# Hybrid decoder layer: last down step by token halves, a later start of Pool's third weight sums, two attention tiles begun at the second pair, compress sum one group later

## The reference

```
h = rmsnorm(x);  x = x + 0.5 * swiglu(h, w_gate, w_up, w_down)      # FFN 0, inner width 2816
h = rmsnorm(x);  x = x + concat(gated_delta_net(h), sparse_attention(h)) @ w_out
h = rmsnorm(x);  x = x + 0.5 * swiglu(h, ...)                        # FFN 1
return rmsnorm(x)                                                    # final norm, then y goes out
```

## Time and profile before

| | |
|---|---|
| median of 3 runs | 1134.47 us (1133.08 to 1135.31) |
| the profiled execution | 1136.39 us, span from first to last instruction 1134.6 us |
| PE busy | 1087.9 us (96%) |
| DVE busy | 777.8 us (69%) |
| ACT busy | 448.7 us (40%) |
| POOL busy | 449.8 us (40%) |
| mean granted TensorE clock | 0.985 |
| DMA | 98.45 MB, 87 GB/s on average |

### The profile page before, as it was taken

One profiled execution on the slowest core, in us unless ns is written; L12 is line 12 of the kernel. 1 busy time (PEld: TensorE's weight loads), 2 busy tenths in 40 slices (PEclk: granted clock), 3 DMA queues, 4 the chain that ended last, 5 costly groups with the idle time before them and its releaser, 6 DMA issues.

```text
span 1134.6 us, 20093 instructions
## 1 busy us (share of the span) xinstructions
PE 1087.9 (96%) x8476; PEld 942.7 (83%) x8476; DVE 777.8 (69%) x926; ACT 448.7 (40%) x628; POOL 449.8 (40%) x288
## 2 busy tenths in 40 slices
PE   6889999999999999899999899999989999999996
PEld 5789899989998888787787567888888899989985
DVE  5998379936986666544456387566997489937963
ACT  6543245413444334311223476343443144413431
POOL 0662169506822000213201299432561279306912
PEclk9999999999999999899999899999999999999998
DMA  6244233332323221123102001123223223322222
GB/s 225 74 124 146 75 108 94 133 100 87 102 84 116 94 77 69 38 74 115 39 31 63 21 2 39 31 82 106 67 88 111 84 103 111 126 98 78 100 84 75
DMA packets 33438, 98.45 MB, mean 87 GB/s; under 512 B 3536, under 2 KB 8144, under 8 KB 31696
## 3 DMA queue, kind: packets, MB, share of 16 engines
q1 hardware_dynamic: 33072, 97.26, 26.1%
q10 hardware_dynamic: 288, 0.08, 0.0%
HBM read 95.24 MB, written 2.10 MB: 86 GB/s over the span
## 4 chain that ended last, share of the span: by engine, by line
PE 87%; DVE 8%; ACT 3%; issue 2%; POOL 0%; DMA 0%; DVEq 0%; ACTq 0%
PE bank L586 24%; PE bank L587 24%; PE bank L588 24%; PE bank L1998 3%; PE bank L1753 1%; PE bank L1784 1%; PE bank L1769 1%; DVE hb_lo L710 1%; DVE w_lo L982 1%; DVE w_lo L905 1%; DVE cv L1498 1%; PE bank L2056 1%; DVE c_sb L1038 1%; PE bank L2053 1%; DVE act_lo L1077 1%
## 5 line engine op out<-in xcount | busy, mean ns | idle before, releaser
L586 PE MATMUL bank<-hb_hi,w_hi 128*128 128x256 f32 x1064 | 295.4, 278 | 13.2 <-DVE w_lo L905 9.3
L587 PE MATMUL bank<-hb_lo,w_hi 128*128 128x256 f32 x1064 | 294.5, 277 | 0.0
L588 PE MATMUL bank<-hb_hi,w_lo 128*128 128x256 f32 x1064 | 294.4, 277 | 0.0
L586 PEld LDWEIGHTS bank<-hb_hi,w_hi 128*128 128x128 f32 x1064 | 200.5, 188 | 14.9 <-issue 6.5
L587 PEld LDWEIGHTS bank<-hb_lo,w_hi 128*128 128x128 f32 x1064 | 200.5, 188 | 0.3
L588 PEld LDWEIGHTS bank<-hb_hi,w_lo 128*128 128x128 f32 x1064 | 200.3, 188 | 0.0
L586 PE MATMUL bank<-act_hi,w_hi 128*128 128x512 f32 x448 | 178.7, 399 | 9.9 <-DVE w_lo L918 9.9
L587 PE MATMUL bank<-act_lo,w_hi 128*128 128x512 f32 x448 | 178.1, 398 | 0.0
L588 PE MATMUL bank<-act_hi,w_lo 128*128 128x512 f32 x448 | 177.9, 397 | 0.0
L899 ACT ACTIVATE w_hi<-raw 128x1536 fp32r<-128x1536 f32 (+1 forms) x67 | 108.8, 1624 | 165.4 <-PE bank L588 165.4
L905 DVE TENSOR_TENSOR w_lo<-raw,w_hi 128x1536 fp32r<-128x1536 f32 (+1 forms) x67 | 158.1, 2360 | 16.0 <-ACT w_hi L899 15.3
(11 more groups left out here) (299 smaller groups left out, 1717.9 us busy)
## 6 DMA issues: line engine op xcount, KB each, us to landing
raw<-in_gate_up SPq DMA_DIRECT2D x43, 1024.0 KB, 5.4
raw<-in_w_in SPq DMA_DIRECT2D x13, 1024.0 KB, 4.9
raw<-in_down SPq DMA_DIRECT2D x8, 1024.0 KB, 5.1
raw<-in_down SPq DMA_DIRECT2D x16, 512.0 KB, 4.2
raw<-in_down SPq DMA_DIRECT2D x8, 768.0 KB, 4.3
raw<-in_w SPq DMA_DIRECT2D x8, 512.0 KB, 4.0
x<-in_x SPq DMA_DIRECT2D x4, 512.0 KB, 7.4
raw<-in_w_out SPq DMA_DIRECT2D x4, 512.0 KB, 4.6
```

Of the source, the lines that this page charges most:

```text
L586: pe.matmul(out_ap, wh, xh, start=first, stop=False)
L587: pe.matmul(out_ap, wh, xl, start=False, stop=False)
L588: return pe.matmul(out_ap, wl, xh, start=False, stop=last)
```

## The change

1. The last `Down` step of the second FFN is done for tokens 0 to 255, then for 256 to 511, each half in a bank of its own, with 256-column matmuls. Additions, squares, POOL's last addition, feature sums, root, reciprocal, broadcast, final multiplication and output DMAs are done per half: 16 multiplications and 16 DMAs of 256 tokens. PE does half 0's feature sums between the two output tiles of half 1. ACT takes a root of one number first. POOL adds the last tile but one per half, too.
2. In both FFNs POOL waits, before the sums of the sixth gate-up step, for the first DVE addition of the fourth one.
3. PE calls `pe_tile_start` for the first two token tiles right after the scores of the second pair, not ahead of their first value products.
4. `hid_sum` and `kcvc` stand one group number later.

```diff
-CMP_AT = {22: ("hid_sum",), 24: ("kcvc",), 26: ("scores", 0), 27: ("scores", 1), 30: ("scores", 2),
+CMP_AT = {23: ("hid_sum",), 25: ("kcvc",), 26: ("scores", 0), 27: ("scores", 1), 30: ("scores", 2),
...
+            if st is FFN[1][-1]:
+                pe_last_down(pe, st)
+                return
...
+        def pe_last_down(pe, st):
+            par = st.step % 2
+            for half in range(2):
+                t = tok_half(half)
+                for ab in range(2):
+                    for j in range(st.tiles):
+                        w = slice((ab * st.tiles + j) * P, (ab * st.tiles + j + 1) * P)
+                        mm = three_pass(pe, last_bank(ab, half), w_hi[:, par, w], w_lo[:, par, w],
+                                        act_hi[:, j, t], act_lo[:, j, t], j == 0, j == st.tiles - 1)
+                    mm.then_inc(last_part, 1)
+                    if half and not ab:
+                        pe_last_sum(pe, 0)
+            pe_last_bc(pe, 0)
+            pe_last_sum(pe, 1)
+            pe_last_bc(pe, 1)
...
+        def pe_last_sum(pe, half):
+            out = spare_bank(half)
+            pe.wait_ge(x_added, X_ADDED0[1] + KT * len(PARTS) - 2)
+            pe.wait_ge(last_summed, half + 1)
+            for src, first in ((sq_sum, True), (sq[:, 1, :], False)):
+                if not first:
+                    pe.wait_ge(last_sq, 2 * half + 2)
+                for i in range(2):
+                    t = 2 * half + i
+                    mm = pe.matmul(out[:, i:i + 1], src[:, t * P:(t + 1) * P], ones,
+                                   start=first and i == 0, stop=not first and i == 1)
+            mm.then_inc(last_ss, 1)
...
+        def dve_last(dve):
...
+            add(0, 0)
+            add(0, 1)
+            add(1, 0)
+            root(0)
+            add(1, 1)
+            for k in range(KT // 2):
+                scaled(0, k)
+            root(1)
+            for k in range(KT // 2, KT):
+                scaled(0, k)
+            for k in range(KT):
+                scaled(1, k)
+
+        def act_last(act):
+            st = FFN[1][-1]
+            act.activation(root_first, eps_col, ACT.Sqrt)
...
+            square(0, 0)
+            square(0, 1)
+            square(1, 0)
+            root(0)
+            square(1, 1)
+            root(1)
+
+        def pool_last(pool):
+            for half in range(2):
+                t = tok_half(half)
+                pool.wait_ge(last_sq, 2 * half + 1)
+                pool.tensor_tensor(sq_sum[:, t], sq_sum[:, t], sq[:, 0, t], ALU.add).then_inc(last_summed, 1)
...
             pool_first_sums(pool, FFN[f][PLAIN + 1])
+            pool.wait_ge(post_done, 5 * FFN[f][PLAIN].n + 1)
             for st in FFN[f][PLAIN + 2:]:
...
+            if i == 1:
+                pe.wait_ge(cmp_pt_evac, 2)
+                for t in range(TT):
+                    if TILE_AT[t] < 2:
+                        pe_tile_start(pe, t)
...
-                if i - PV_LAG == TILE_FIRST[t]:
-                    if i == PV_LAG:
-                        pe.wait_ge(cmp_pt_evac, 2)
-                    if TILE_AT[t] >= 2:
-                        pe.wait_ge(ocat_lo, TILE_AT[t] - 1)
+                if i - PV_LAG == TILE_FIRST[t] and TILE_AT[t] >= 2:
+                    pe.wait_ge(ocat_lo, TILE_AT[t] - 1)
                     pe_tile_start(pe, t)
...
-            for k in range(KT):
-                sp.wait_ge(y_ready, k + 1)
-                sp.dma_start(out[:, k, :], x[:, k, :]).then_inc(out_landed, 16)
+            for half in range(2):
+                t = tok_half(half)
+                for k in range(KT):
+                    sp.wait_ge(y_ready, half * KT + k + 1)
+                    sp.dma_start(out[:, k, t], x[:, k, t]).then_inc(out_landed, 16)
```

More of the change, by code:

```diff
@@ L881, in pe_down, with last_bank, spare_bank, tok_half @@
                                         act_hi[:, j, :], act_lo[:, j, :], j == 0, j == st.tiles - 1)
-                    if st is FFN[1][-1] and ab == 0:
-                        mm.then_inc(last_half, 1)
             mm.then_inc(step_done, 1)
+        def last_bank(ab, half):
+            return banks[4 * (FFN[1][-1].step % 2) + 2 * half + ab][:, 0:TOK]
+        def spare_bank(i):
+            return banks[4 * (1 - FFN[1][-1].step % 2) + i]
+        def tok_half(half):
+            return slice(half * TOK, (half + 1) * TOK)
@@ new lines, in pe_last_bc, with add, root, scaled @@
+        def pe_last_bc(pe, half):
+            pe.wait_ge(last_rstd, half + 1)
+            for i in range(2):
+                t = 2 * half + i
+                mm = pe.matmul(spare_bank(2 + half)[:, i * P:(i + 1) * P], rstd[:, t:t + 1].to_broadcast([P, P]), ident,
+                               start=True, stop=True)
+            mm.then_inc(last_bc, 1)
+        def dve_last(dve):
+            st = FFN[1][-1]
+            def add(half, ab):
+                k, t = 2 * st.at + ab, tok_half(half)
+                dve.wait_ge(last_part, 2 * half + ab + 1)
+                dve.scalar_tensor_tensor(x[:, k, t], last_bank(ab, half), 0.5, x[:, k, t], ALU.mult, ALU.add)\
+                   .then_inc(last_added, 1)
+            def root(half):
+                c = slice(2 * half, 2 * half + 2)
+                dve.wait_ge(last_rms, half + 1)
+                dve.reciprocal(rstd[:, c], rms[:, c]).then_inc(last_rstd, 1)
+            def scaled(half, k):
+                t = tok_half(half)
+                if k == 0:
+                    dve.wait_ge(last_bc, half + 1)
+                    dve.wait_ge(last_added, 2 * half + 2)
+                dve.scalar_tensor_tensor(x[:, k, t], x[:, k, t], norm_w[:, 3, k:k + 1],
+                                         spare_bank(2 + half)[:, 0:TOK], ALU.mult, ALU.mult).then_inc(y_ready, 1)
+            add(0, 0)
[10 more added lines that the diff above has]
+                scaled(1, k)
@@ L1022, in act_ffn @@
                     act_split_sums(act, then)
-                if isinstance(st, Down) and st.part == len(PARTS) - 1:
+                if isinstance(st, Down) and st.part == len(PARTS) - 1 and st is not FFN[1][-1]:
                     for k in (2 * st.at, 2 * st.at + 1):
@@ L1100, in dve_ffn @@
                     dve_split_sums(dve, then, 1)
-                if isinstance(st, Down):
+                if isinstance(st, Down) and st is not FFN[1][-1]:
                     for ab in range(2):
                         k = 2 * st.at + ab
[L1104 to L1107, removed]
+                        dve.wait_ge(step_done, splits(st.step) + 1)
                         dve.scalar_tensor_tensor(x[:, k, :], banks[4 * (st.step % 2) + ab][:, :], 0.5, x[:, k, :],
@@ L1122, in pool_sums @@
             pool_clear(pool, m)
-            for k in range(KT - 1):
+            for k in range(KT - 2 if m == 3 else KT - 1):
                 pool.wait_ge(sq_ready, (m - 1) * KT + k + 1)
```

33 lines of the change are left out of this document (23 added, 10 removed).

## The result

The changed kernel took 1126.16 us (median of 8 runs, 1122.70 to 1128.46), the kernel before beside it 1134.07 (8 runs, 1130.95 to 1136.60). The ratio is 0.9924, 95% interval 0.9908 to 0.9941: 8.6 us faster (6.7 to 10.4; the two medians by themselves lie 7.9 apart), where 14.6 were forecast. The profiled execution took 1126.86 us (span 1125.1), 9.5 less than the one of before.

The account below looks back on a forecast made before the run. PE was taken as the bound, busy 96% of the span, leaving waits, low clock and the tail to win. Terms 3.8 + 1.0 + 3.1 + 3.2 + 3.5 = 14.6 us off 1134.5 gave 1119.9, forecast 1120; range 1115 to 1126.

Parts of the forecast that it names:

- Pool's wait, first FFN: Sixth gate-up step, first FFN: PE's wait of 3.36 us becomes 2.4, worth 1.0 us (-0.5 to 2.2).
- Pool's wait, second FFN: Sixth gate-up step, second FFN: PE's wait falls from 5.4 to about 2.4 us; worth 3.8 us (1.5 to 5.5).
- compress sum: Mixer: PE's 1.49 us wait for evictions and 1.7 us of lower clock behind it go; 3.1 us (0.8 to 3.3).
- tile starts: Attention: two tile starts fit into PE's 4.47 us wait for the first exponentials; 3.2 us (1.2 to 4.2).
- tail: Kernel's end: half 0's chain finishes beside half 1's matmuls, so the last multiplication ends earlier; 3.5 us (0 to 4.5).
- rival E: Mixer: compress sum and tile starts both gain nothing because they find another wait; 1126.2 us, chance 0.04.
- C: FFN starts: Pool/VectorE lock time is only moved; 1123.2 us, or 1126.9 with lower clock and low attention gain; together 0.18.
- A: The forecast itself, all places gaining as priced: 1119.9 us, chance 0.62.
- B: Tail bound by SP's output issues (16 x 0.65 us) or smaller transfers, its 3.5 us lost; 1123.4 us, chance 0.13.
- The half of the low clock behind this wait: Second FFN, behind PE's sixth-step wait: 1.5 us of lower clock may or may not come; half, 0.8 us, counted.
- the lost clock: Attention, behind the wait for exponentials: of 3.4 us lost to low clock, 0.4 us goes as idle time shrinks.
- I take DVE's pace: Output at the end: SP's 16 DMA issues were assumed to follow DVE's multiplications, not cost 0.65 us each (10.3 us).

Follow-up runs that it names:

- e1: The kernel before with only Pool's wait ahead of its sums added, in both FFNs: 1131.01 us, ratio 0.9967.
- e2: The kernel before with only the compress sum and its copies one group later: 1132.44 us, ratio 0.9974.
- e7: The changed kernel plus eight 512-wide matmuls of zeros behind the two early tile starts, filling the attention's remaining wait: 1121.66 us, ratio 0.9877.
- e4: The kernel before with only the last down step by token halves and halved output DMAs: 1131.57 us, ratio 0.9983.
- e10: The changed kernel with tile starts back at their old places and the attention's 4.5 us wait filled with 20 matmuls of zeros: 1123.63 us, ratio 0.9899.
- e8: The changed kernel with the last output in 8 DMAs of two tiles instead of 16 of one: 1124.06 us, ratio 0.9899.

## Why the prediction was right and wrong

| term | predicted | between the two profiles | alone on the chip (interval) |
|---|---|---|---|
| Pool's wait, first FFN | 1.0 | 1.6 | both: |
| Pool's wait, second FFN | 3.8 | 3.3 | 3.7 (1.9 to 5.6) |
| compress sum | 3.1 | 3.1 | 3.0 (1.0 to 4.9) |
| tile starts | 3.2 | -0.8 | -0.6 (-2.5 to 1.2) |
| tail (2.1 from the last `Down` step on) | 3.5 | 2.3 | 1.9 (-0.1 to 4.0) |
| sum | 14.6 | 9.5 | 8.0; all together 8.6 |

The direction was right, and three of the four places gave something; the size was not right, and 1126.16 lies just above the upper end of the range (1126). It is also rival E's number, 1126.2, and that is luck: E has the compress sum bring nothing, and it brought its 3.1. C's later time, 1126.9, lies outside the range that is said to hold C, and the chances of A, B, C and E add up to 0.97, not 0.96; neither bears on the forecast.

- **Pool's wait** held: the operations ahead of L1059 are back at 1.21 us, PE's wait at the sixth step is 2.03 us (2.4 predicted) in the second FFN and 1.01 in the first, and it did not come back at the seventh step. Rival C, 1.5 us in all because the stretches only move, lies below the interval of e1. The step's flaw: it took one profile's order of VectorE and Pool as certain. The predicted 4.8 against 3.7 alone is inside the interval; e2's trace shows how a loss there can be absent without the edit. The half of the low clock behind this wait, 0.8 of the 3.8, did not show: from PE's start at the sixth step to the first addition of the next `Down` step it is 41.47 us before, with the low clock, 41.34 in the changed kernel, without it but at TensorE's slower pace (0.118 us from matmul to matmul, last section), and 40.39 in e7, which has neither. The prediction's own 0.110 counts matmuls that reach over the ends of a window; the timelines show 0.113, which moves no term.
- **Compress sum** held in both halves, wait and clock, and the scores did not feel the later copies. Its clock half is luck in part: e4 had the wait and no low clock.
- **Tile starts: this step failed.** "With 2.0 instead of 4.5 us idle some of the 3.4 us of lost clock goes too: 0.4". The wait shrank as predicted (4.47 to 1.88), the two starts ran in 1.4 us each instead of 2.1 and 1.25, but the lost clock grew. The 3.4 us were priced by length and not by place: part of that spell lay in the wait, for nothing, and the step moved it onto products and got a longer one. The prediction has that low clock "just behind a wait", but in the trace of before it is already 0.50 from 642.90 on, 1.1 us ahead of the scores at 643.98 (0.80 in the earlier trace rows shows it too). The starts are worth 1.5 us with no low clock (e10 against e7), a term of 2.1 + 0.7 at mixed clock in the prediction. Why the spell was 10.2 us and not 6.8 is open. Rival E named the effect (nothing gained) with the wrong cause, another wait.
- **Tail: two sizes in this step failed.** The multiplications began 0.45 us after the last addition started (5.32 in the earlier trace rows), as forecast. But they ran at (1.65 + 4.77) / 16 = 0.40 us each, where the step took 5.35 / 16 = 0.33 and set 0.42 aside: 6.42 us in all instead of 5.35 + 0.18, 0.9 more. And "I take DVE's pace" failed for SP: an issue costs 0.48 us, so the issues end at 1123.30, 1.8 us behind the last multiplication, one of the things the prediction said would show it wrong. From the last multiplication's end to the end of the span it is 2.7 us before and 3.6 after, another 0.9. The way to the first multiplication came out some 0.4 us better than forecast, so 2.1 of the 3.5 were left. Rival B was right in its mechanism, at 0.48 instead of the 0.65 that it took from the earlier trace rows; its loss is 1.0 to 1.4 us and not all of the 3.5.

## What to carry to other kernels

A wait that can't be removed is also the cheapest place for the low clock: look at the length of the first matmuls behind it, and before moving work into a part of it, ask where the clock will then be low; filling what was left of the wait with zeros brought 4.5 us over the changed kernel, and 2.7 over the kernel without early starts (medians). Neither half does it alone: the early starts without the fill lost what they gave, the fill without the early starts brought 0.75 (1.6 in the trace). Count the DMA issues when a transfer is halved: once an issue (0.48 us) is longer than the operation that feeds it (0.40 us), the queue is the end of the kernel. A gain read from one profile of a stretch in which VectorE and Pool take turns is a gain against one of several orders; what an edit that fixes the order is worth is read from many runs.

## What the runs showed beyond that

- TensorE has two paces at the same granted clock of 1.00. In 12 us the changed kernel did 104 matmuls of 256 columns and e7 did 108 (windows 838 to 850 of both), 0.118 and 0.113 us from start to start in the timelines, in the same code. From PE's start at the sixth step of the second FFN to the next `Down` step it makes 0.95 us (41.34 against 40.39); the pace changes where PE has waited, and which one comes next differs between executions. What decides it is open.
- Ahead of the tail the low clock came in the traces in spells of 3.4 to 10.2 us, at the same few places (behind the waits at 54, 461, 549, 640 and 834 us, and at 393, where PE does 16 one-column sums), and which of them an execution has differs. It is likely a part of the spread between runs of one kernel, from 1.9 us (six runs of e8) to 9.4 (twelve of e2), but that is not shown: e8, whose wait is not filled, spreads less than e7 (2.5 us, six runs).
